# Two-layer mixer on one core: remaining modulation parameters summed per partition on VectorE in the projections, over partitions in the Fourier stage

## The reference, cut to what matters

```python
D_MODEL = 1024; SEQ = 1024; DEPTH = 2; CTX_LEN = 256; F_GROUPS = 4

def ada_params(cvec, w, b):
    m = jax.nn.silu(cvec) @ w + b            # w: 1024 x 3072 per layer
    return jnp.split(m, 3, axis=-1)          # shift, scale, gate

def modulate(x, g, shift, scale):
    return rms_norm(x, g) * (1.0 + scale) + shift

def fourier_mix(u):                          # u: 1024 rows, 4 groups of 128 channels
    f = jnp.fft.fftn(u32, axes=(1, 3), norm="ortho").real

for i in range(DEPTH):
    shift, scale, gate = ada_params(c, ada_w[i], ada_b[i])
    h = modulate(x_lat, norm_g[i], shift[:, None, :], scale[:, None, :])
    # i = 0: h @ w_in gives f, q, k, v and the gate columns; Fourier mix of f, attention of q, k, v
    # i = 1: short convolution mixer
    x_lat = x_lat + gate[:, None, :] * y
```

## Time and profile before

| what | value |
|---|---|
| median of 3 runs | 1843.58 us (1843.51 to 1847.05) |
| time of the profiled execution | 1843.34 us |
| its span in the profile | 1840.8 us |
| PE busy | 1771.6 us, 96% of the span |
| DVE busy | 1174.0 us, 64% |
| ACT busy | 796.0 us, 43% |
| POOL busy | 757.5 us, 41% |
| mean granted PE clock | 0.986 |

### The profile page before, as it was taken

The page is one execution under the profiler, slowest core; times in us unless marked ns, Lnnn a source line. Parts: engine busy times, 40 slices in busy tenths (PEclk is TensorE's granted clock), DMA queues, the critical chain, the costliest instruction groups (busy, mean ns, idle before and its releaser), DMA issues.

```text
span 1840.8 us, 23052 instructions
## 1 busy us (share of the span) xinstructions
PE 1771.6 (96%) x8789; PEld 1473.6 (80%) x8789; DVE 1174.0 (64%) x1328; ACT 796.0 (43%) x1248; POOL 757.5 (41%) x450
## 2 busy tenths in 40 slices
PE   6999999889999899999999999999999999989999
PEld 4788888668888788788888888987888888878887
DVE  3740983448898814864545653597666666779876
ACT  3522121446766523633333532745443444444443
POOL 2322422000000032466666521357999999910000
PEclk8999999999999899999999999999999999999999
DMA  9511112640000272022212341312323222286433
GB/s 360 191 57 47 47 58 80 258 168 1 0 0 1 84 237 69 24 80 69 81 57 68 127 137 46 110 29 80 92 81 92 80 91 81 69 309 245 142 120 121
DMA packets 165384, 188.32 MB, mean 102 GB/s; under 512 B 9454, under 2 KB 117543, under 8 KB 165159
## 3 DMA queue, kind: packets, MB, share of 16 engines
q1 hardware_dynamic: 165287, 187.00, 30.8%
HBM read 152.37 MB, written 34.60 MB: 102 GB/s over the span
## 4 chain that ended last, share of the span: by engine, by line
PE 52%; DVE 4%; ACT 2%; issue 1%; DMA 1%; SPq 0%; ACTq 0%; DVEq 0%
PE ps L3152 20%; PE ps L2160 14%; PE ps L3203 10%; PE ps L2220 5%; PE ps L3503 1%; PE ps L3165 1%; DMA y_a<-y_scratch 1%; DVE cv_lo_p L132 1%; DVE up_lo_p L132 1%; DVE residual L2082 0%; ACT residual L3339 0%; PE ps L3169 0%; DVE residual L3061 0%; ACT cv_hi_p L129 0%; ACT residual L1899 0%
## 5 line engine op out<-in xcount | busy, mean ns | idle before, releaser
L3152 PE MATMUL ps<-up_hi_p,st_hi_p 128*128 128x512 f32 x560 | 218.7, 391 | 2.9 <-ACT residual L2870 2.9
L3152 PE MATMUL ps<-up_lo_p,st_hi_p 128*128 128x512 f32 x560 | 218.5, 390 | 0.0
L3152 PE MATMUL ps<-up_hi_p,st_lo_p 128*128 128x512 f32 x560 | 218.3, 390 | 0.0
L3203 PE MATMUL ps<-down_ring 128*128 128x512 f32 x924 | 210.9, 390 | 5.0 <-DVE down_ring L132 4.8
L3203 PEld LDWEIGHTS ps<-down_ring 128*128 128x128 f32 x924 | 173.0, 188 | 42.6 <-issue 3.9
L132 POOL TENSOR_TENSOR in_lo<-in_raw,in_hi 128x512 fp32r<-128x512 f32 (+1 forms) x54 | 93.4, 1736 | 219.0 <-ACT in_hi L129 218.9
L2160 PE MATMUL ps<-cv_hi_p,cv_st_hi_p 128*128 128x512 f32 x392 | 153.2, 391 | 2.7 <-ACT residual L1878 2.7
L2160 PE MATMUL ps<-cv_hi_p,cv_st_lo_p 128*128 128x512 f32 x392 | 153.2, 391 | 0.0
L2160 PE MATMUL ps<-cv_lo_p,cv_st_hi_p 128*128 128x512 f32 x392 | 153.0, 390 | 0.0
L132 POOL TENSOR_TENSOR st_lo_p<-up_raw,st_hi_p 128x512 fp32r<-128x512 f32 x68 | 100.8, 1486 | 65.9 <-ACT st_hi_p L129 65.9
L3152 PEld LDWEIGHTS ps<-up_hi_p,st_hi_p 128*128 128x128 f32 x560 | 105.5, 188 | 25.3 <-issue 3.3
(11 more groups left out here) (381 smaller groups left out, 4203.7 us busy)
## 6 DMA issues: line engine op xcount, KB each, us to landing
up_raw<-in_ffn_w_in SPq DMA_DIRECT2D x44, 512.0 KB, 5.1
w_raw<-in_ffn_w_out SPq DMA_DIRECT2D x66, 256.0 KB, 2.9
ada_raw_rest<-in_ada_w SPq DMA_DIRECT2D x32, 512.0 KB, 6.0
cv_raw<-in_odd_w_in SPq DMA_DIRECT2D x32, 512.0 KB, 5.5
in_raw<-in_even_w_in SPq DMA_DIRECT2D x48, 256.0 KB, 2.8
y_scratch<-residual SPq DMA_DIRECT2D x22, 512.0 KB, 2.6
ada_raw<-in_ada_w SPq DMA_DIRECT2D x16, 512.0 KB, 9.2
residual<-in_x SPq DMA_DIRECT2D x8, 512.0 KB, 9.2
```

What stands on the lines that cost most here:

```text
L3152: last = pe.matmul(ps[:, bank(j, p), :], w[p][:, kk * P:(kk + 1) * P], x[p][:, kk, :], start=(first and w is st_hi and x is up_hi), stop=( ...
L3203: last = pe.matmul(ps[:, 4 * (i % 2) + m, :], slot[:, s, m * P:(m + 1) * P], slot[:, x, :], start=(k == 0 and s == 0 and x == 2 and DOWN[i ...
```

## The change

The diff is cut to its core; "..." marks what is left out.

It takes the 32 loads of the remaining `ada_w`, and the sum over row blocks, out of the Fourier stage and puts them into the projections.

- SP issues two loads of 128x1024 behind each weight slice from slice 28 on (16 slices, 28 to 43). There are two buffers: the `square` tile of the norm and a new tile `rest_odd`; each load waits until DVE has used its buffer.
- DVE multiplies each unit by the conditioning value of its partition and adds it to `rest_sum` (128 x 8 x 512): 4 `tensor_scalar` and 28 `scalar_tensor_tensor` of 128x1024. They stand between the norm of x and the lambda products.
- `hc_hi`/`hc_lo` are placed elsewhere; `rest_sum` lies over them, so DVE first waits for the context's tiles.
- PE sums `rest_sum` over partitions with eight matmuls against ones, behind pair 2 of group 0, and turns the rows behind pair 1 of group 1. DVE copies, adds biases and forms the gain in groups 0 and 1. The column for c_ctx is no longer made for these pieces.
- The first half of each channel product waits for the first two pairs' low parts only, not for all four.

```diff
+            rest_sum = sb(st, "rest_sum", [P, len(ADA_REST), BANK])
+            rest_odd = sb(st, "rest_odd", [P, 2 * BANK])
...
+            hc_hi = sb(st, "hc_hi", [P, KT, CTX], F32R)
+            hc_lo = sb(st, "hc_lo", [P, KT, CTX], F32R)
...
+                rest_raw = [square, rest_odd]
...
+                REST_FROM, REST_PER_SLICE = 28, 2
...
+                        sp.wait_ge(sem("in_x_squared"), RT)
                         sp.wait_ge(sem("xt_copied"), RT)
...
+                        def rest_load(u):
+                            if u >= 2:
+                                sp.wait_ge(sem("rest_added"), u - 1)
+                            l, m = ADA_REST[2 * (u % 4)]
+                            rows = slice(u // 4 * P, (u // 4 + 1) * P)
+                            sp.dma_start(rest_raw[u % 2][:, :], a["ada_w"][l, rows, m * BANK:(m + 2) * BANK])\
+                              .then_inc(sem(f"rest_in{u % 2}"), 16)
...
+                        rest = iter(range(REST_UNITS))
                         for n in range(CTX_SLICES + RING, N_SLICES):
                             load_slice(sp, n)
+                            if n >= REST_FROM:
+                                for _ in range(REST_PER_SLICE):
+                                    u = next(rest, None)
+                                    if u is not None:
+                                        rest_load(u)
...
                         norm_x.vector_scale(dve, 1, KT)
+                        dve.wait_ge(sem("in_tile"), FIRST_TILE["ctx"] + TILES_OF["ctx"])
+                        for u in range(REST_UNITS):
+                            k, j = u // 4, u % 4
+                            part = rest_sum[:, 2 * j:2 * j + 2, :].rearrange("p a n -> p (a n)")
+                            dve.wait_ge(sem(f"rest_in{u % 2}"), 16 * (u // 2 + 1))
+                            if k == 0:
+                                dve.tensor_scalar(part, rest_raw[u % 2][:, :], cond_col[:, k, 0:1], None, ALU.mult)\
+                                   .then_inc(sem("rest_added"), 1)
+                            else:
+                                dve.wait_ge(sem("rest_added"), u - 3)
+                                dve.scalar_tensor_tensor(out=part, in0=rest_raw[u % 2][:, :], scalar=cond_col[:, k, 0:1], in1=part,
+                                                         op0=ALU.mult, op1=ALU.add).then_inc(sem("rest_added"), 1)
...
-                UNITS, N_RAW = 4 * KT, 7
-                ada_raw = sb(st, "ada_raw_rest", [P, N_RAW, 2 * BANK])
...
-                        for u in range(UNITS):
...
-                            if u >= N_RAW:
-                                sp.wait_ge(sem("rest_ada_used"), (u - N_RAW) // 2 + 1)
-                            l, m = ADA_REST[2 * (u % 4)]
-                            rows = slice(u // 4 * P, (u // 4 + 1) * P)
-                            sp.dma_start(ada_raw[:, slot(u), :], a["ada_w"][l, rows, m * BANK:(m + 2) * BANK])\
-                              .then_inc(sem(f"rest_ada_in{slot(u)}"), 16)
...
-                        def ada(n):
...
-                            ada_product(pe, ADA_REST[4 * b:4 * b + 4], 2 + b, k, cond,
-                                        [ada_raw[:, slot(2 * n + i // 2), i % 2 * BANK:(i % 2 + 1) * BANK] for i in range(4)])\
-                                .then_inc(sem("rest_ada_used"), 1)
+                        def rest_summed():
+
+                            pe.wait_ge(sem("first_q_low"), 2)
+                            for i in range(len(ADA_REST)):
+                                j = 32 * (i % 4)
+                                last = pe.matmul(ps[j:j + 32, REST_BANK + i // 4, :], ones[:, 0:32], rest_sum[:, i, :],
+                                                 start=True, stop=True)
+                            last.then_inc(sem("rest_summed"), 1)
...
-                        units_after = (0, 1, 1, 2)
-                        units = iter(range(UNITS // 2))
...
-                                    for _ in range(units_after[k1 // 2]):
-                                        ada(next(units))
-
-                            pe.wait_ge(sem("ft_low"), (g + 1) * PAIRS)
+                                if (g, k1) == (0, 5):
+                                    rest_summed()
+                                if (g, k1) == (1, 3):
+                                    pe.wait_ge(sem("rest_rows"), 1)
+                                    rest_turn(pe, REST_BANK, rest_rows).then_inc(sem("rest_turned"), 1)
+
                             if g == 0:
                                 pe.wait_ge(sem("channel_low"), 1)
...
                             for half in range(2):
                                 k1s = slice(half * PAIRS, (half + 1) * PAIRS)
+                                pe.wait_ge(sem("ft_low"), g * PAIRS + (half + 1) * PAIRS // 2)
...
-                        pe.wait_ge(sem("rest_ada_rows"), 1)
-                        ada_turn(pe, ADA_REST, ada_rows).then_inc(sem("rest_ada_turned"), 1)
...
-                        dve.memset(cond[:, :, :], 0.0).then_inc(sem("rest_cond_zero"), 1)
-                        dve.wait_ge(sem("rest_cond_zero"), 1)
-                        dve.tensor_copy(cond[:, :, 0:2], cond_col[:, :, :]).then_inc(sem("rest_cond_ready"), 1)
...
-                        dve.wait_ge(sem("rest_ada_used"), UNITS // 2)
-                        dve.tensor_copy(ada_rows[:, :, :], ps[:, 2:4, :]).then_inc(sem("rest_ada_rows"), 1)
-                        dve.wait_ge(sem("rest_ada_turned"), 1)
-                        ada_bias(dve, ADA_REST).then_inc(sem("rest_ada_cols"), 1)
-                        dve.wait_ge(sem("rest_ada_cols"), 1)
-                        ada_gain(dve, 2, 1, 0)
+                            if g == 0:
+                                dve.wait_ge(sem("rest_summed"), 1)
+                                dve.tensor_copy(rest_rows[:, :, :], ps[:, REST_BANK:REST_BANK + 2, :]).then_inc(sem("rest_rows"), 1)
+                            if g == 1:
+                                dve.wait_ge(sem("rest_turned"), 1)
+                                rest_bias(dve, REST_BANK).then_inc(sem("rest_cols"), 1)
+                                dve.wait_ge(sem("rest_cols"), 1)
+                                ada_gain(dve, 2, 1, 0)
```

More of the change, by code:

```diff
@@ L276, in program, with rest_turn, rest_bias @@
         ADA_REST = [(0, 4), (0, 5)] + [(1, m) for m in range(6)]
[L278 to L284, removed]
-            return last
[L287 to L295, removed]
+        REST_UNITS = len(ADA_REST) // 2 * KT
+        def rest_turn(pe, first_bank, rows):
+            for b in range(len(ADA_REST) // 4):
+                for t in range(4):
+                    last = pe.transpose(ps[:, first_bank + b, t * P:(t + 1) * P], rows[:, b, t * P:(t + 1) * P], ident[:, :])
+            return last
+        def rest_bias(dve, first_bank):
+            for i, (l, m) in enumerate(ADA_REST):
                 b = ADA_B[1] + l * ADA_T + 4 * m
                 j = 32 * (i % 4)
-                last = dve.tensor_tensor(ada_col[:, l, 4 * m:4 * m + 4, :],
-                                         ps[:, i // 4, :].rearrange("p (t n) -> p t n", n=P)[:, :, j:j + 2],
-                                         cols[:, ADA_B[0], b:b + 4].unsqueeze(2).broadcast_to([P, 4, 2]), ALU.add)
+                last = dve.tensor_tensor(ada_col[:, l, 4 * m:4 * m + 4, 0:1],
+                                         ps[:, first_bank + i // 4, :].rearrange("p (t n) -> p t n", n=P)[:, :, j:j + 1],
+                                         cols[:, ADA_B[0], b:b + 4].unsqueeze(2), ALU.add)
             return last
@@ L405, in program @@
         FOLDED = (7, 3, 1, 4, 0, 5, 2, 6)
+        with ExitStack() as st:
+            sb(st, "below_rest", [P, 4 * D])
+            rest_sum = sb(st, "rest_sum", [P, len(ADA_REST), BANK])
+            rest_odd = sb(st, "rest_odd", [P, 2 * BANK])
+        with ExitStack() as st:
+            sb(st, "below_context", [P, 4 * D])
+            hc_hi = sb(st, "hc_hi", [P, KT, CTX], F32R)
+            hc_lo = sb(st, "hc_lo", [P, KT, CTX], F32R)
         def even_projections():
@@ L993, in fourier @@
                 ft_hi, ft_lo = (sb(st, "ft_" + part, [P, RADIX, 2, P], F32R) for part in ("hi", "lo"))
[L996 to L1002 removed]
+                rest_rows = sb(st, "rest_rows", [P, 2, BANK])
+                REST_BANK = 2
                 def group_input(g):
@@ L1023, in _ @@
                         sp.dma_start(channel_dft[:, :, :], a["channel_dft"]).then_inc(sem("channel_in"), 16)
-                        for u in range(UNITS):
-                            if slot(u) == 0 and u < N_RAW:
-                                sp.wait_ge(sem("first_q_turned"), 2)
-                            if u >= N_RAW:
-                                sp.wait_ge(sem("rest_ada_used"), (u - N_RAW) // 2 + 1)
-                            l, m = ADA_REST[2 * (u % 4)]
-                            rows = slice(u // 4 * P, (u // 4 + 1) * P)
```

(14 more changed lines are left out.)

4 lines of the change are left out of this document (removed).

## The result

The changed kernel took 1850.8 us as the median of 17 runs (1845.07 to 1857.88), the kernel before 1842.89 us in the 17 runs beside them (1835.94 to 1847.8). The ratio is 1.0049, with a 95% interval of 1.0037 to 1.006: 7 to 11 us slower. The predicted time was 1849.8, the range 1844.5 to 1861. The profiled execution took 1848.63 us, with a span of 1846.6 (5.8 more than before) and a mean clock of 0.981 against 0.986.

A forecast was written before the change was run, and what follows sets the result against it. It took PE, with 52% of the chain of waits, as the bound, and ACT's in-order root as what holds PE up. From 1843.34 us, -10 + 15 + 1.5 = +6.5 gave 1849.8, range 1844.5 to 1861.

The forecast's parts named there:

- The Fourier gain: Fourier stage: taking 16 steps off PE shortens a group's period from 12.2 us, gaining 10 us, between 9 and 14.
- ACT's way out: Fourier stage: with PE's steps gone, ACT's output is late next; y_f starts 3.3 us after pair 3 ends, instead of 5.0.
- The last unit: Projections: DVE finishes the last of 32 units at 187 us, between 186 and 190, paced by SP's loads.
- The landing: Projections: a unit's load takes 4.2 us to land, with 3.6 and 6.0 as bounds.
- up to a us of waiting for its buffer: Projections: the last unit's allowance for a busy buffer; a turn of 5.5 us against a slice's 5.44 keeps SP on pace.
- The k root: ACT's root of the k norms, behind DVE's 14.4 us of squares, ends at 202.5 us instead of 181.47.
- The first stop: Projections: PE waits 5 to 11 us ahead of slice 40, which starts at 205 to 210 us instead of 199.5.
- The second stop counts: Gate step 2: the q root comes 15.0 us late, PE has no cover, costing 15 us, between 14 and 18.
- The clock: PE's lower granted clock after the stop ahead of gate step 2 adds 1.5 us, with 0 and 3 as bounds.
- Cover holds: Rival: DVE's idle 52.1 and 38.8 us swallow the units, only the 10 us gain remains, 1833 us; chance 8%.
- Slow loads: Rival: loads in the projections cannot keep pace, last unit at 217 us, total 1880, or 1865 if milder; chance 12%.
- The port rule: Projections: POOL and DVE hold each other off, priced at nothing; without slack another 20 us, 1870, chance 2%.

The follow-up runs named there:

- run 1: Changed kernel with only the first four of the 32 units loaded and multiplied, the new Fourier stage kept: 1832.39 us, 0.9946 of the kernel before.
- Run 8: Kernel of run 3, but PE waits for all four low parts of a Fourier group before either half of y_f: 1841.2 us, ratio 0.9992.
- run 2: Changed projections with all 32 loads, ahead of the Fourier stage of the kernel before: 1865.03 us, 1.0128 of the kernel before.
- run 9: Changed kernel with DVE's folding of f moved behind the scaling and rotation of q: 1842.01 us, 1.0002 of the kernel before.
- run 11: Changed kernel with the lambda products ahead of the units and nothing else: 1854.47 us in 4 runs, 1.0064 of the kernel before.
- run 5: Changed kernel in its own order, loads starting with slice 24 instead of 28: 1843.23 us, 1.0001 of the kernel before.
- run 3: Changed kernel with lambda products ahead of the units and rows of k squares between them: 1834.07 us, 0.9953 of the kernel before.
- run 10: Changed kernel with the order of run 3 and the folding of f behind q: 1832.69 us, 0.9951 of the kernel before.
- run 6: Changed kernel with only four loads issued, all 32 units multiplied and added from what the buffers hold: 1831.45 us, 0.9946 of the kernel before.

## Why the prediction was right

**The Fourier gain**, -10: measured 10.05 in the trace and 10 alone (run 1). The period came out at 9.2 (9.1 to 9.4 was worked out), `y_f` 3.1 us behind `ft_hi` of pair 3 (3.3 from its end). Run 8 splits it: the half wait carries 5.5 of it. The prediction's remark that "ACT's way out" is late next was the important one.

**The last unit**, 187: this was the term that was mis-sized. Counted from the high part of slice 39 (177.65 before, 174.48 after), the forecast was 9.4 us and the trace shows 13.7. The landing was right (4.2 forecast, 4.2 and 4.3 measured); the estimate of 3.2 us by the Trainium skill was too short. The Trainium skill, "DMA: Bandwidth & Descriptors", section "Anatomy of one DMA — SWDGE (gpsimd) path", gives that sum for transfers issued by GpSimd. These loads went out on SP's hardware queue. The measurement decides. What failed was "up to a us of waiting for its buffer". A buffer's turn is 4.3 + 1.3 = 5.6, over a slice's 5.44; the units went by at (186.94 - 99.91) / 31 = 2.81 us, and the last load waited for its buffer until 182.64, where the forecast, moved by the 3.2 us, has 177.3. SP did fall behind, by 0.1 to 0.2 us a slice, some 2.6 in all. Another 1.1 us came from the unit that POOL held up at 175.15. In the other three executions with this order and these loads the last unit ended 12.1 us (run 2), 12.0 (run 9) and 13.8 (run 11) behind the high part of slice 39. Only run 11 has a unit that was held near the end too (172.10, 2.35 us). So the slow turn accounts for some 12 us (9.4 + 2.6) and the hold-up for most of the rest; this is read from the four traces, and no run tried it.

**The k root**, its end forecast at 202.5: 203.61, that is 4.3 us later against the slices. The 14.4 us of squares were right: 188.80 to 203.2.

**The first stop**, 5 to 11: 9.66, but not by the way that led to the upper bound. POOL was not held up: its low part of slice 40 took 1.27 us and started at 204.21, ahead of DVE's product (204.34). What PE waited for last were ACT's copies of f, which the forecast does not name. Its 9.66 are nearly the lower bound and the 4.3 us by which the root was late. Its low clock was covered by the second stop, as forecast: both only move PE's arrival at step 2, where it waited 7.72 anyway (3 to 7 was forecast).

**The second stop counts**: right, and runs 5 and 9 show it from both sides. Without the first stop, the loss up to step 2 was still 7. The reason is that PE has no slack at step 2, so the projections lose what the q root is late. Against the slices, that is 273.34 - 256.87 + 3.2 = 19.7, where +15.0 was forecast; the 4.4 of the last unit explain nearly all of the difference. In runs 2 and 11 the same count gives 17.8 and 19.0. Between the two roots two errors cancel, which is luck: from the k root to the end of the folding DVE took 58.1 us instead of 56.1, and for the squares of q 11.6 instead of 13.3.

**The clock**, +1.5: 1.5 behind the second stop. 19.7 + 1.5 = 21.2 against the 21.0 found at the stage's end.

**Sum.** Forecast: -10 + 15 + 1.5 = +6.5. Trace: -10.05 + 21.0 = +11 counted from slice 16, 7.7 with the early start. Over all runs the ratio gives 7 to 11, its middle 9.0, 2.5 above the forecast and in the direction of the mis-sized term. So the mechanism was right, but that the median of 1850.8 lies only 1 us from 1849.8 is luck.

**The rivals.** "Cover holds" would have been right with one other order (runs 3 and 10): DVE's 52 us really do swallow 41 us of additions, but only if the squares that ACT waits for don't stand behind them. Slow loads did not come. The port rule had next to no price on POOL, as the 1319 ns show. Its other half, "POOL holds DVE by 1.2", was priced at nothing and cost about 1.1 us on the way to the last unit in this execution, since units that wait for their buffer have no slack.

## What to carry to other kernels

Before work is put into an engine's idle time, ask what stands behind it in that engine's list and who has a deadline on it; put the waited-for work ahead of, or between, the new pieces. Where one late chain feeds two deadlines, the later, tighter one sets the total: the two stops and the first one's clock (9.66 + 7.72 + 1.5) came to nearly what the q root was late (19.7). What is won at the first stop alone should then be waited for at the second; this follows from the times, and no run tried it with the q root left where it was. With two buffers, filler that must keep up with something else needs a turn (landing and use) clearly under that pace; a third buffer would be the obvious thing to try, and was not tried.

## What the runs showed of the hardware

The opening of the kernel has two courses. In the window 44 to 48 us the granted clock was 0.83 in the profile before, and 1.00 in that of the change (the first and the second row):

```profile
44.00:48.00 4.00, 2.75 (x12) 2.44 (x13) 3.69 (x9) 2.44 (x5) 0.75 (x2) 0.83 1.02 401
```

```profile
44.00:48.00 4.00, 4.00 (x27) 3.29 (x25) 3.78 (x8) 2.91 (x5) 1.66 (x3) 1.00 1.02 400
```

Slice 16 started at 64.4 to 65.7 in the change and runs 1, 2, 6 and 9, and at 66.7 to 68.1 in the seven others, though run 5 differs from the change in nothing ahead of 68 us (67.67 against 64.36). So 3 us between two profiles can belong to the execution and not to the edit, and times of two profiles should be compared from a common event, not from zero. Of the kernel before there is one profile only, so whether it opens early in other executions isn't known. What decides between the two was not tried.

POOL and DVE held each other off. Behind the first stop POOL's low parts of slices 41 and 42 took 6.54 us each beside DVE's two products of 128x5120; those of slices 40 and 43 to 45 took 1.3 to 1.5:

```profile
205.44 6.54 POOL L132 TENSOR_TENSOR in_lo<-in_raw,in_hi 128x512 fp32r<-128x512 f32 x1
```

Short instructions were held too: the unit at 175.15 took 2.42 us instead of 1.28, and a rotation product of DVE at 241.87 took 2.67 instead of 0.42 beside POOL's low part at 241.86 (2.40 us). The Trainium skill, "SBUF — State Buffer", section "Who interferes with whom", describes this exclusion, and the trace agrees. Beside the units it mostly fell on POOL, which had slack, and cost nothing there; where it fell on a unit, it came out at the end of the chain.
